# Second attention of a two-block model on one core: the differential heads' bias rows written out by GpSimd, so that VectorE adds bias and takes the maximum in one instruction per softmax

## The chip, the core and the metric

The kernel runs as one launch on one core of a Trainium2 chip. Its time is the device time of that core in microseconds (us); before and after are compared by their medians. The engines are TensorE (PE in the profile, PEld for its weight loads), VectorE (DVE), ScalarE (ACT), GpSimd (POOL) and SyncE (SP, which here only issues DMAs). Each works through its own queue in order and waits on semaphores.

## The reference, cut to what matters

A first block (sparse attention, memory attention, SwiGLU) and a second block follow each other. The second block has four MLA heads and then four differential heads. Of the latter, for one head and 128 queries (`Q_BLOCK`) against all 1024 keys:

```python
bucket = _t5_bucket_2(kpos[None, :] - qpos[:, None])
bias = jnp.moveaxis(table[bucket], -1, 0)
s = jnp.einsum('bqhmd,bkhmd->bmhqk', qblk, k).astype(jnp.float32) * scale + bias
p = jax.nn.softmax(s, axis=-1)
a = p[:, 0] - lam * p[:, 1]
return jnp.einsum('bhqk,bkhd->bqhd', a.astype(v.dtype), v)
```

The bucket depends only on key position minus query position, and it is constant once that distance is 128 or more on either side. So for 128 queries the bias varies over at most 384 keys (the block's own 128 and 128 on each side); to the left and to the right of them it is one number per head.

## The kernel before, in words

The stage is cut into 64 units: one head times 128 queries. Units 0 to 31 are the MLA heads, 32 to 63 the differential heads; I call the latter d0 to d31 here. Within a differential head the query block is i = 0 to 7. Four units form a group; a group's probabilities are transposed and multiplied with the values together.

A differential unit goes through the engines like this. TensorE writes the logits of both softmaxes (m = 0, 1) to PSUM (`ps`, function `logits`, L1915/L1916); each may start when VectorE has read the former unit's logits of the same m (semaphore `e_red`). VectorE adds the bias, writes the row to SBUF (`rows` for m = 0, `second` for m = 1) and takes the maximum (`maxima`, L3724). ScalarE takes both exponentials (L2742). VectorE forms the difference of the two rows (`difference`: reciprocal L3738, a 128x1 product L3739, the 128x1024 product and sum L3740; both of the latter read two SBUF operands). TensorE transposes the four rows of a group, once all four differences are there (L1930), ScalarE copies them (L2750), and TensorE multiplies them with the values (L1942). VectorE's order is written out by hand: the difference of unit u-1 stands behind the maxima of unit u, except at the first unit of a group, where it stands ahead of them.

In the MLA heads VectorE has another duty instead, the rounded rest of the transposed probabilities (`pt_lo`, L3759). The last MLA group's rests fall among the maxima of d1 to d3.

The bias of a head is a tile of 128x384 (`e_bias`, two buffers), brought by SP (L698). SP issues twelve half-tile loads of the head's queries and keys first (L695), then the bias; from the third differential head on it also waits until the head two before has been read (`e_red`). The far bias is a column of that tile read with stride 0. A row of 1024 keys is therefore two or three instructions: left of the near keys, right of them, and the near keys. i = 0, 1, 6 and 7 have two pieces, i = 2 to 5 have three. A short reduction over the pieces' maxima follows (L3729).

GpSimd splits weights and MLA operands into a rounded part and a rest: `w_hi` (L785) adds zero to `w_raw`, and `w_lo` (L788) subtracts. Behind the last MLA head it splits the first two slabs of the output projection `out_2`, and then waits for the third until the attention is over.

Of the kernel before, what the change touches and what calls it, by code (L numbers as in the profile page):

```python
# [21 lines left out]
ALU = mybir.AluOpType  # L22
AX = mybir.AxisListType

P = 128
D = 1024
KT = D // P
S = 1024
NT = S // P
# [28 lines left out]
TAKEN = -3e38  # L58
# [65 lines left out]
def program(nc, t):  # L124

    out = t["out"]
    with ExitStack() as ctx:
# [4 lines left out]
        KB = 1024  # L132
# [4 lines left out]
        BR = AR + 64 * KB  # L137
# [3 lines left out]
        def at(name, offset, shape, dt=F32):  # L141
            return nc.alloc_sbuf_tensor_at(name, shape, dt, offset=offset)
# [20 lines left out]
        zero = small("zero", [P, 1])  # L163
# [117 lines left out]
        second = [at(f"second{i}", tmp_at + 4 * KB * i, [P, S]) for i in range(2)]  # L281
        o_stage = at("o_stage", late_at, [P, HALF])
        inverses = at("inverses", late_at + 2 * KB, [P, 4, P])
        e_bias = at("e_bias", late_at + 4 * KB, [P, 2, 3 * P])
        e_stat = at("e_stat", late_at + 7 * KB, [P, 8, 6, 2])
        o_in = at("o_in", BR, [P, KT, S])
        o_rms = [at(f"o_rms{i}", BR + 40 * KB + 4 * KB * i, [P, S]) for i in range(2)]
# [22 lines left out]
        def wide(slot):  # L310

            return ps[:, 2 * slot:2 * slot + 2, :].rearrange("p b n -> p (b n)")
# [113 lines left out]
        def splits_before(hd):  # L426

            return 10 * hd
# [125 lines left out]
        def _(sp):  # L554
# [126 lines left out]
            for d in range(DIFF_HEADS):  # L681
                hd, p = MLA_HEADS + d, head_parts[d % 2]
                q_hi, q_lo = (t["diff_qk"][part, d] for part in range(2))
                k_hi, k_lo = (t["diff_qk"][part, d + DIFF_HEADS] for part in range(2))
                sp.wait_ge(a_qk, NT * (hd - 1) + NT * max(0, d - 1))
                sp.wait_ge(heads_in, heads_landed(hd))
                if d == 0:
                    sp.wait_ge(head_split, splits_before(MLA_HEADS))
                for dst, lanes, src in ((p[0], top, q_hi[top]), (p[0], bottom, q_lo[top]),
                                        (p[1], top, q_lo[bottom]), (p[1], bottom, q_hi[bottom]),  # L690
                                        (p[2], top, k_hi[top]), (p[2], bottom, k_hi[top]),
                                        (p[7], top, k_lo[top]), (p[7], bottom, k_lo[top]),
                                        (p[3], top, k_hi[bottom]), (p[3], bottom, k_hi[bottom]),
                                        (p[8], top, k_lo[bottom]), (p[8], bottom, k_lo[bottom])):
                    sp.dma_start(dst[lanes, :].bitcast(F32), src).then_inc(heads_in, 16)  # L695
                if d >= 2:
                    sp.wait_ge(e_red, 16 * (d - 1))
                sp.dma_start(e_bias[:, d % 2, :], t["bias_tiles_2"][d]).then_inc(bias_2_in[d % 2], 16)  # L698
                sp.wait_ge(a_pv, 16 * (hd - 1))
                sp.dma_start(v_plain[d % 2][:], t["diff_v"][d].rearrange("p j n -> p (j n)")).then_inc(heads_in, 16)  # L700
            load_slabs(SLABS["out_2"][0] + 2, N_SLABS)
# [77 lines left out]
        def _(pool):  # L779
# [29 lines left out]
            def split_front_first(n):  # L809

                s, front, back = n % 2, slice(0, HALF), slice(HALF, 1024)
                hi, lo = w_hi[s], w_lo[s]
                pool.wait_ge(raw_landed[s], loaded(n))
                pool.wait_ge(front_used, FRONT_FIRST.index(n) + 1)
                step(nc.gpsimd.tensor_tensor(hi[:, front], raw[s][:, front], zero[:, 0:1].broadcast_to([P, HALF]), ALU.add))  # L815
                nc.gpsimd.tensor_tensor(lo[:, front], raw[s][:, front], hi[:, front].bitcast(F32),
                                        ALU.subtract).then_inc(front_split, 1)
                pool.wait_ge(w_used, n - 1)
                nc.gpsimd.tensor_tensor(hi[:, back], raw[s][:, back], zero[:, 0:1].broadcast_to([P, HALF]),
                                        ALU.add).then_inc(w_rounded, 1)  # L820
                pool.wait_ge(w_rounded, n + 1)
                nc.gpsimd.tensor_tensor(lo[:, back], raw[s][:, back], hi[:, back].bitcast(F32),
                                        ALU.subtract).then_inc(w_split, 1)

            def split_next(n):

                pool.wait_ge(w_used, n - 1)
                pool.wait_ge(raw_landed[n % 2], loaded(n))
                split(n % 2, n + 1)
# [218 lines left out]
            for hd in range(MLA_HEADS):  # L1048
# [48 lines left out]
                pool.wait_ge(head_split, splits_before(hd) + 9)  # L1097
                rest(2, p[5], both)
            pool.wait_ge(head_split, splits_before(MLA_HEADS))
            first = SLABS["out_2"][0]  # L1100
            split_next(first)
            split_next(first + 1)
            split_front_first(first + 2)
            split_next(first + 3)
            split_slabs(first + 4, N_SLABS)
# [1911 lines left out]
        def _(dve):  # L3017
# [683 lines left out]
            def maxima(unit):  # L3701
                g, q, d = unit // 4 % 2, unit % 4, unit - NT * MLA_HEADS
                if d < 0:
                    dve.wait_ge(a_qk, unit + 1)
                    nc.vector.tensor_reduce(mstat[:, g, 1, q:q + 1], wide(unit % 2), AX.X, ALU.max,
                                            negate=True).then_inc(a_max, 1)
                    return

                i, bias = unit % NT, e_bias[:, d // NT % 2, :]
                if i == 0:  # L3710
                    dve.wait_ge(bias_2_in[d // NT % 2], 16 * (d // NT // 2) + 16)
                near0, near1 = max(0, i - 1) * P, min(NT, i + 2) * P
                b0 = P if i == 0 else 0
                stats = e_stat[:, unit % 8]
                dve.wait_ge(a_tr, 2 * (unit - unit % 4) - 8)
                if d >= 2:
                    dve.wait_ge(a_probs, d - 1)
                for m, row in enumerate((prob_rows[g][q], second[unit % 2])):
                    dve.wait_ge(a_qk, NT * MLA_HEADS + 2 * d + m + 1)
                    for kind, lo, hi, b in ((0, 0, near0, bias[:, 0:1].broadcast_to([P, near0])),  # L3720
                                            (2, near1, S, bias[:, 3 * P - 1:3 * P].broadcast_to([P, S - near1])),
                                            (1, near0, near1, bias[:, b0:b0 + near1 - near0])):
                        if lo < hi:
                            ins = nc.vector.tensor_tensor_reduce(row[:, lo:hi], wide(m)[:, lo:hi], b, 1.0, TAKEN,  # L3724
                                                                 ALU.add, ALU.max, stats[:, kind, m:m + 1])
                    ins.then_inc(e_red, 1)
                dve.wait_ge(e_red, 2 * d + 2)
                kinds = slice(0 if near0 else 1, 3 if near1 < S else 2)
                nc.vector.tensor_reduce(stats[:, 3, :], stats[:, kinds, :].rearrange("p k m -> p m k"), AX.X, ALU.max,  # L3729
                                        negate=True).then_inc(a_max, 1)  # L3730

            def difference(unit):

# [476 lines left out]
```

## Time and profile before

| what | value |
|---|---|
| median of 3 runs | 3044.64 us (3044.28 to 3047.01) |
| the profiled execution's own time | 3047.95 us |
| its span | 3046.2 us |
| TensorE busy | 2923.9 us (96%) |
| VectorE busy | 2043.8 us (67%) |
| GpSimd busy | 1607.7 us (53%) |
| differential units' maxima | from 2112.0 to about 2271.6 us of the span |

Busy shares are averages over stages with different limits, and TensorE's ends are modelled. All times of a row are in us from the span's start, durations in us unless marked ns. In a timeline, a bracket at a row's end is the time that the engine sat idle before it, and what ended it.

### The profile page before, as it was taken

Reading aid. Unit: us, or ns where it says so; the run is one execution under the profiler, and the core shown is the slowest. Engines: PE = TensorE matmul, PEld = TensorE weight load, DVE = VectorE, ACT = ScalarE, POOL = GpSimd, SP = SyncE. Lnnn points to the kernel's source line nnn. Section 1 sums busy time; section 2 is a strip of 40 time slices with the busy share of each in tenths; the row PEclk is TensorE's granted clock in tenths of the full one; section 3 lists DMA queues with packets and bytes.
Section 4 is the critical chain, followed back from the end, with each engine's and each line's share of the span. In section 5 each row is a group of like instructions: output and inputs, shape, how many; then the busy total and the mean of one; then the engine's idle time right before and its main releaser. Section 6 shows DMA issues by size and latency. Waiting matters only on the chain.

```text
span 3046.2 us, 39303 instructions
## 1 busy us (share of the span) xinstructions
PE 2923.9 (96%) x12850; PEld 2297.7 (75%) x12850; DVE 2043.8 (67%) x3010; ACT 1246.5 (41%) x2024; POOL 1607.7 (53%) x1015
## 2 busy tenths in 40 slices
PE   9999998999989999999999999999999899999998
PEld 7788775668877778887787677587657688877886
DVE  7899975546276977777548532456984766666658
ACT  4321215620246644444222432455774566652221
POOL 3254333324442388888679234471002477777877
PEclk9999999999999999999999999999999999999999
DMA  3122310025121144445974122624422277788774
GB/s 124 39 90 97 144 57 21 1 88 206 52 76 49 73 173 163 164 164 193 373 263 148 51 98 95 207 80 109 116 83 67 89 263 262 261 334 334 264 254 172
DMA packets 156608, 449.31 MB, mean 148 GB/s; under 512 B 17084, under 2 KB 28516, under 8 KB 155720
## 3 DMA queue, kind: packets, MB, share of 16 engines
q1 hardware_dynamic: 128656, 369.68, 34.9%
q10 hardware_dynamic: 27832, 78.08, 6.9%
q8 instruction: 69, 1.13, 0.2%
q14 instruction: 51, 0.42, 0.0%
HBM read 298.25 MB, written 148.13 MB: 147 GB/s over the span
## 4 chain that ended last, share of the span: by engine, by line
PE 74%; DVE 9%; issue 6%; POOL 5%; ACT 3%; DMA 2%; SPq 0%; ACTq 0%; POOLq 0%; DVEq 0%
PE ps L1223 21%; PE ps L1225 20%; PE ps L1224 20%; POOL left_lo L896 2%; PE ps L1466 2%; PE ps L1942 1%; PE ps L1930 1%; PE ps L1273 1%; POOL part_in L891 1%; DVE sums_t L3509 1%; PE ps L1456 1%; PE ps L1915 1%; PE ps L1916 1%; DVE score L3102 0%; DVE tmp L3040 0%
## 5 line engine op out<-in xcount | busy, mean ns | idle before, releaser
L896 POOL TENSOR_TENSOR left_lo<-part_in,left_hi 128x512 fp32r<-128x512 f32 x414 | 576.3, 1406 | 254.9 <-ACT left_hi L2843 89.6
L891 POOL TENSOR_TENSOR part_in<-part_in,part_in 128x512 f32<-128x512 f32 x252 | 364.0, 1445 | 35.8 <-DMA part_in<-mlp_weights_dram 15.0
L785 POOL TENSOR_TENSOR w_hi<-w_raw,zero 128x1024 fp32r<-128x1024 f32 x65 | 127.5, 1962 | 424.3 <-PE ps L1225 419.9
L1223 PE MATMUL ps<-h_hi,w_hi 128*128 128x512 f32 x480 | 188.4, 393 | 5.7 <-DVE h_lo L3034 5.7
L1224 PE MATMUL ps<-h_lo,w_hi 128*128 128x512 f32 x480 | 187.3, 390 | 0.0
L1225 PE MATMUL ps<-h_hi,w_lo 128*128 128x512 f32 x480 | 187.3, 390 | 0.0
L788 POOL TENSOR_TENSOR w_lo<-w_raw,w_hi 128x1024 fp32r<-128x1024 f32 x65 | 181.3, 2790 | 5.1
L3127 DVE MATCH_REPLACE8 score<-top,score 128x1024 f32<-128x1024 f32 (+2 forms) x192 | 180.5, 1020 | 0.0
L815 POOL TENSOR_TENSOR w_hi<-w_raw,zero 128x512 fp32r<-128x512 f32 x4 | 5.6, 1398 | 329.9 <-PE ps L1225 329.9
L1223 PE MATMUL ps<-down_t,left_hi 128*128 128x512 f32 x432 | 170.9, 396 | 8.4 <-DVE part_t L3414 4.1
L3123 DVE MAX8 top<-score 128x8 f32<-128x1024 f32 (+2 forms) x192 | 174.6, 1022 | 0.0
L1224 PE MATMUL ps<-down_t,left_hi 128*128 128x512 f32 x432 | 169.7, 393 | 0.0
L1225 PE MATMUL ps<-down_t,left_lo 128*128 128x512 f32 x432 | 169.6, 393 | 0.0
L2863 ACT ACTIVATE left_hi<-part_in 128x512 fp32r<-128x512 f32 x96 | 59.1, 630 | 201.8 <-PE ps L1225 175.6
L1223 PE MATMUL ps<-sums_hi,left_hi 128*128 128x512 f32 x320 | 126.4, 395 | 5.8 <-POOL left_lo L896 4.7
L2496 ACT ACTIVATE left_hi<-part_in 128x512 fp32r<-128x512 f32 x140 | 84.7, 626 | 104.0 <-DMA part_in<-ffn_weights_dram 40.3
L1225 PE MATMUL ps<-sums_hi,left_lo 128*128 128x512 f32 x320 | 125.3, 392 | 0.0
L1224 PE MATMUL ps<-sums_lo,left_hi 128*128 128x512 f32 x320 | 125.1, 391 | 0.0
L1223 PE MATMUL ps<-normed_hi,w_hi 128*128 128x512 f32 x272 | 116.7, 429 | 5.4 <-DVE normed_lo L3591 4.3
L1223 PEld LDWEIGHTS ps<-h_hi,w_hi 128*128 128x128 f32 x480 | 90.4, 188 | 26.5 <-DVE h_lo L3034 7.7
L876 POOL TENSOR_TENSOR mix_rows<-mix_rows,stat 128x128 f32<-128x128 f32 (+7 forms) x48 | 54.9, 1146 | 103.5 <-DVE stat L3168 103.4
L1224 PE MATMUL ps<-normed_lo,w_hi 128*128 128x512 f32 x272 | 106.7, 392 | 0.0
(640 smaller groups left out, 8739.4 us busy)
## 6 DMA issues: line engine op xcount, KB each, us to landing
w_raw<-weights_dram SPq DMA_DIRECT2D x102, 512.0 KB, 3.3
part_in<-ffn_weights_dram SPq DMA_DIRECT2D x144, 256.0 KB, 3.3
part_in<-mlp_weights_dram SPq DMA_DIRECT2D x144, 256.0 KB, 4.5
mlp_parts_scratch<-part_t SPq DMA_DIRECT2D x64, 512.0 KB, 4.7
down_t<-mlp_parts_scratch SPq DMA_DIRECT2D x64, 512.0 KB, 6.5
ffn_parts_scratch<-part_t SPq DMA_DIRECT2D x44, 512.0 KB, 4.7
down_t<-ffn_parts_scratch SPq DMA_DIRECT2D x44, 512.0 KB, 6.3
mlp_parts_scratch<-part_b SPq DMA_DIRECT2D x32, 512.0 KB, 5.1
```

Of the source, the lines that this page charges most:

```text
L785: nc.gpsimd.tensor_tensor(w_hi[s][:], raw[s][:], zero[:, 0:1].broadcast_to([P, 1024]), ALU.add).then_inc(w_rounded, 1)
L788: nc.gpsimd.tensor_tensor(w_lo[s][:], raw[s][:], w_hi[s][:].bitcast(F32), ALU.subtract).then_inc(w_split, 1)
L891: tt(part_in[p][dst][:], part_in[p][dst][:], part_in[p][other][:], ALU.add).then_inc(left_summed, 1)
L896: tt(lo[:], src[:], hi[:].bitcast(F32), ALU.subtract).then_inc(w_split, 1)
L1223: nc.tensor.matmul(out, sh, mh, start=start, stop=False)
L1224: nc.tensor.matmul(out, sh, ml, start=False, stop=False)
L1225: return nc.tensor.matmul(out, sl, mh, start=False, stop=stop)
L1466: nc.tensor.matmul(ps[:, 6 + group % 2, :], value[:, j, :], probs_t[n_tr % 2][:], start=j == 0, stop=j == group // 2).then_inc(pv_done, 1)
L2496: nc.scalar.activation(left[i % 4][0][:], part_in[p][RAW_OF_UP[i]][:], ACT.Copy).then_inc(w_rounded, 1)
L2863: nc.scalar.activation(left[j % 4][0][:], src[:], ACT.Copy).then_inc(w_rounded, 1)
L3123: nc.vector.max(top8[:, e, :], sc).then_inc(dve_step, 1)
L3127: nc.vector.match_replace(sc, top8[:, e, :], sc, TAKEN).then_inc(dve_step, 1)
```

## The change

`e_bias` becomes a full row of 2S - P = 1920 columns per head, at another place in SBUF. SP writes the same 384 columns, now into its middle (columns 768 to 1151). GpSimd fills the 768 columns on each side with the neighbouring column (`far_biases`), so that every query block i finds its 1024 bias values as one slice, from column (7 - i)·128 on. VectorE then needs one instruction per softmax, and the maxima of both are negated by a small multiplication instead of the reduction. A semaphore step of 18 instead of 16 makes VectorE wait for both fills. The fills of heads 0 and 1 stand on GpSimd's queue ahead of the first two slabs of `out_2`, those of heads 2 and 3 behind them.

```diff
-        e_bias = at("e_bias", late_at + 4 * KB, [P, 2, 3 * P])
+        BIAS_SPAN, NEAR_AT = 2 * S - P, S - 2 * P
+        e_bias = at("e_bias", BR + 36 * KB, [P, 2, BIAS_SPAN])
...
-                sp.dma_start(e_bias[:, d % 2, :], t["bias_tiles_2"][d]).then_inc(bias_2_in[d % 2], 16)
+                sp.dma_start(e_bias[:, d % 2, NEAR_AT:NEAR_AT + 3 * P], t["bias_tiles_2"][d]).then_inc(bias_2_in[d % 2], 16)
...
+            def far_biases(d):
+
+                e = d % 2
+                pool.wait_ge(bias_2_in[e], 18 * (d // 2) + 16)
+                for lo, hi, col_of in ((0, NEAR_AT, NEAR_AT), (NEAR_AT + 3 * P, BIAS_SPAN, NEAR_AT + 3 * P - 1)):
+                    nc.gpsimd.tensor_tensor(e_bias[:, e, lo:hi], e_bias[:, e, col_of:col_of + 1].broadcast_to([P, hi - lo]),
+                                            zero[:, 0:1].broadcast_to([P, hi - lo]), ALU.add).then_inc(bias_2_in[e], 1)
+
+            far_biases(0)
+            far_biases(1)
             first = SLABS["out_2"][0]
             split_next(first)
             split_next(first + 1)
+            far_biases(2)
+            far_biases(3)
             split_front_first(first + 2)
...
-                    dve.wait_ge(bias_2_in[d // NT % 2], 16 * (d // NT // 2) + 16)
-                near0, near1 = max(0, i - 1) * P, min(NT, i + 2) * P
-                b0 = P if i == 0 else 0
+                    dve.wait_ge(bias_2_in[d // NT % 2], 18 * (d // NT // 2) + 18)
+                row0 = (NT - 1 - i) * P
...
-                    for kind, lo, hi, b in ((0, 0, near0, bias[:, 0:1].broadcast_to([P, near0])),
-                                            (2, near1, S, bias[:, 3 * P - 1:3 * P].broadcast_to([P, S - near1])),
-                                            (1, near0, near1, bias[:, b0:b0 + near1 - near0])):
-                        if lo < hi:
-                            ins = nc.vector.tensor_tensor_reduce(row[:, lo:hi], wide(m)[:, lo:hi], b, 1.0, TAKEN,
-                                                                 ALU.add, ALU.max, stats[:, kind, m:m + 1])
-                    ins.then_inc(e_red, 1)
+                    nc.vector.tensor_tensor_reduce(row[:], wide(m), bias[:, row0:row0 + S], 1.0, TAKEN,
+                                                   ALU.add, ALU.max, stats[:, 1, m:m + 1]).then_inc(e_red, 1)
                 dve.wait_ge(e_red, 2 * d + 2)
-                kinds = slice(0 if near0 else 1, 3 if near1 < S else 2)
-                nc.vector.tensor_reduce(stats[:, 3, :], stats[:, kinds, :].rearrange("p k m -> p m k"), AX.X, ALU.max,
-                                        negate=True).then_inc(a_max, 1)
+                ts(stats[:, 3, :], stats[:, 1, :], -1.0, None, ALU.mult).then_inc(a_max, 1)
```

GpSimd's queue behind the last MLA head (`head_part` is that head's last split, `w_hi`/`w_lo` the slabs of `out_2`), before:

```order
L1068 TENSOR_TENSOR head_part_5_231<-head_raw_214,head_part_4_230 128x1024 [waits head_split]
L785 TENSOR_TENSOR w_hi_51<-w_raw_49,zero 128x1024 [waits raw_landed0,w_used,head_split]
L788 TENSOR_TENSOR w_lo_53<-w_raw_49,w_hi_51 128x1024 [waits w_rounded]
L785 TENSOR_TENSOR w_hi_52<-w_raw_50,zero 128x1024 [waits raw_landed1,w_used]
L788 TENSOR_TENSOR w_lo_54<-w_raw_50,w_hi_52 128x1024 [waits w_rounded]
L815 TENSOR_TENSOR w_hi_51<-w_raw_49,zero 128x512 [waits front_used,raw_landed0]
```

And the same place of the queue after:

```order
L1069 TENSOR_TENSOR head_part_5_231<-head_raw_214,head_part_4_230 128x1024 [waits head_split]
L1107 TENSOR_TENSOR e_bias<-e_bias,zero 128x768 [waits bias_2_in0,head_split]
L1107 TENSOR_TENSOR e_bias<-e_bias,zero 128x768
L1107 TENSOR_TENSOR e_bias<-e_bias,zero 128x768 [waits bias_2_in1]
L1107 TENSOR_TENSOR e_bias<-e_bias,zero 128x768
L786 TENSOR_TENSOR w_hi_51<-w_raw_49,zero 128x1024 [waits raw_landed0,w_used]
L789 TENSOR_TENSOR w_lo_53<-w_raw_49,w_hi_51 128x1024 [waits w_rounded]
L786 TENSOR_TENSOR w_hi_52<-w_raw_50,zero 128x1024 [waits raw_landed1,w_used]
L789 TENSOR_TENSOR w_lo_54<-w_raw_50,w_hi_52 128x1024 [waits w_rounded]
L1107 TENSOR_TENSOR e_bias<-e_bias,zero 128x768 [waits bias_2_in0]
```

The two slabs' splits (four instructions) now stand behind the second head's bias (`bias_2_in1`), so they cannot start before its load has landed.

VectorE's queue at d3, a unit with three pieces per row (`rows_3` is m = 0, `second_252` is m = 1; the 128x1 rows write the maximum out), before:

```order
L3724 ISA rows_3_246,e_stat<-ps,e_bias 128x256 [waits attn_logits,attn_probs,attn_transposed]
L3724 ISA e_stat 128x1
L3724 ISA rows_3_246,e_stat<-ps,e_bias 128x384
L3724 ISA e_stat 128x1
L3724 ISA rows_3_246,e_stat<-ps,e_bias 128x384
L3724 ISA e_stat 128x1
L3724 ISA second_252,e_stat<-ps,e_bias 128x256 [waits attn_logits]
```

And from the same unit after, on to the differences of d2 and d3 and the first row of d4:

```order
L3733 ISA rows_3_246,e_stat<-ps,e_bias 128x1024 [waits attn_logits,attn_probs,attn_transposed]
L3733 ISA e_stat 128x1
L3733 ISA second_252,e_stat<-ps,e_bias 128x1024 [waits attn_logits]
L3733 ISA e_stat 128x1
L3736 TENSOR_SCALAR e_stat<-e_stat 128x2 [waits attn_biased]
L3765 TENSOR_TENSOR pt_lo<-ps,pt_hi 128x512 [waits attn_probs_t_hi] x2
L3744 RECIPROCAL e_stat<-e_stat 128x1 [waits attn_exp]
L3745 SCALAR_TENSOR_TENSOR e_stat<-e_stat,stat 128x1 [waits dve_step]
L3746 SCALAR_TENSOR_TENSOR rows_2_245<-second_251,e_stat,rows_2_245 128x1024 [waits dve_step]
L3744 RECIPROCAL e_stat<-e_stat 128x1 [waits attn_exp]
L3745 SCALAR_TENSOR_TENSOR e_stat<-e_stat,stat 128x1 [waits dve_step]
L3746 SCALAR_TENSOR_TENSOR rows_3_246<-second_252,e_stat,rows_3_246 128x1024 [waits dve_step]
```

Six pieces of the unit became two instructions of 1024 columns; what stands behind them keeps its order.

## Rows read from the trace of the kernel before

**Rows 1.** The page: share of the chain that ended last, by engine.

```profile
PE 74%; DVE 9%; issue 6%; POOL 5%; ACT 3%; DMA 2%; SPq 0%; ACTq 0%; POOLq 0%; DVEq 0%
```

**Rows 2.** The chain in order of time, d2 to d4: start, duration, what.

```profile
2120.58 1.29 DVE pt_lo L3759 x2
...
2139.52 0.50 PE ps L1915
```

**Rows 3.** The same chain, at a later group's first unit (d12).

```profile
2176.69 0.55 DVE rows L3724
...
2180.62 1.72 PE ps L1942 x4
```

**Rows 4.** Timeline of VectorE, from d1's difference to d4: start, duration, instruction.

```profile
2127.82 0.22 DVE L3739 SCALAR_TENSOR_TENSOR e_stat<-e_stat,stat 128x1 f32<-128x1 f32 x1
2128.08 1.28 DVE L3740 SCALAR_TENSOR_TENSOR rows<-second,e_stat,rows 128x1024 f32<-128x1024 f32 x1
2129.50 0.42 DVE L3724 CUSTOM_DVE_ANT_0 rows<-ps,e_bias 128x256 f32<-128x256 f32 x1
...
2130.80 0.42 DVE L3724 CUSTOM_DVE_ANT_0 second<-ps,e_bias 128x256 f32<-128x256 f32 x1
...
2136.78 0.55 DVE L3724 CUSTOM_DVE_ANT_0 rows<-ps,e_bias 128x384 f32<-128x384 f32 x1
...
2175.03 0.16 DVE L3738 RECIPROCAL e_stat<-e_stat 128x1 f32<-128x1 f32 x1 [1.23 <-ACT second L2742]
```

**Rows 5.** Groups by shape, VectorE, 2100 to 2290: count, busy us, mean ns.

```profile
L3724 DVE CUSTOM_DVE_ANT_0 rows<-ps,e_bias 128x384 f32<-128x384 f32 x32 | 17.4, 552 | 0.0
L3724 DVE CUSTOM_DVE_ANT_0 rows<-ps,e_bias 128x768 f32<-128x768 f32 x8 | 7.6, 954 | 0.5
```

**Rows 6.** Timeline of TensorE: the longer idle times, and value products behind the last.

```profile
2136.93 1.09 PE L1930 MATMUL ps<-ident,rows 128*128 128x128 f32 x8 [1.68 <-DVE rows L3740]
2276.64 1.09 PE L1930 MATMUL ps<-ident,rows 128*128 128x128 f32 x8 [2.09 <-DVE rows L3740]
2278.07 3.48 PE L1942 MATMUL ps<-pt_plain,v_plain 128*128 128x512 f32 x4 [0.34 <-ACT pt_plain L2750]
```

**Rows 7.** Windows of 1 us: length, busy of five engines, granted clock, DMA.

```profile
2278.00:2279.00 1.00, 0.93 (x1) 0.50 (x2) 0.00 (x0) 0.42 (x1) 0.00 (x0) 0.50 1.03 418
```

**Rows 8.** SP's timeline at the second head's bias; its load's row, KB, us to landing.

```profile
2115.85 0.59 SPq L698 DMA_DIRECT2D e_bias<-bias_tiles_scratch  x1
e_bias<-bias_tiles_scratch SPq DMA_DIRECT2D x1, 192.0 KB, 10.0
```

**Rows 9.** Timeline of GpSimd: the second slab's split, and a 128x512 rounding.

```profile
2067.39 1.90 POOL L785 TENSOR_TENSOR w_hi<-w_raw,zero 128x1024 fp32r<-128x1024 f32 x1
2069.38 2.41 POOL L788 TENSOR_TENSOR w_lo<-w_raw,w_hi 128x1024 fp32r<-128x1024 f32 x1
2311.17 1.04 POOL L815 TENSOR_TENSOR w_hi<-w_raw,zero 128x512 fp32r<-128x512 f32 x1 [239.39 <-PE ps L1225]
```

**Rows 10.** Timelines of VectorE and GpSimd near 1831, and the same VectorE instruction alone.

```profile
1830.30 1.90 POOL L785 TENSOR_TENSOR w_hi<-w_raw,zero 128x1024 fp32r<-128x1024 f32 x1 [7.54 <-PE ps L1225]
1831.31 1.97 DVE L3660 TENSOR_TENSOR d_out<-d_out,d_hi 128x1024 f32<-128x1024 f32 x1
1832.27 3.23 POOL L788 TENSOR_TENSOR w_lo<-w_raw,w_hi 128x1024 fp32r<-128x1024 f32 x1
...
1864.56 1.22 DVE L3660 TENSOR_TENSOR d_out<-d_out,d_hi 128x1024 f32<-128x1024 f32 x1 [1.13 <-ACT d_hi L2683]
```

**Rows 11.** Short instructions beside GpSimd; by line: ns min/median/max, first and last start.

```profile
494.95 0.83 POOL L876 TENSOR_TENSOR mix_rows<-mix_rows,stat 128x384 f32<-128x384 f32 x1 [2.93 <-DVE stat L3168]
495.47 0.32 DVE L3163 TENSOR_TENSOR stat<-stat 128x1 f32<-128x1 f32 x1
...
L3164 DVE TENSOR_SCALAR stat<-stat x64: 153/154/156, 476.5 to 634.6; 128x1 f32<-128x1 f32 x64
L3759 DVE TENSOR_TENSOR pt_lo<-ps,pt_hi x64: 680/682/693, 1986.2 to 2132.9; 128x512 fp32r<-128x512 f32 x64
```

## The prediction

> **What bounds the kernel now.** I read the page's chain first: TensorE holds 74% of it, VectorE 9% [rows 1]. The change touches only the differential heads, so I followed the chain in order of time through that stage. It has two kinds of stretch. From d2 to d4 it lies on VectorE without a break, from the first `pt_lo` at 2120.58 to the logits that TensorE starts at 2139.52 [rows 2]: the last MLA group's rests and three units of maxima come together there, and TensorE waits, 1.68 us ahead of the first differential group's transposes [rows 6]. Later TensorE sets the pace inside a group, and only the step from one group to the next runs over the others: ScalarE's exponentials, the difference, then both rows of the next unit's maxima, until TensorE has its second logits and goes on to the values [rows 3]. There VectorE is idle for 1.23 us for the last exponential [rows 4], so what it saves earlier in a group is worth nothing. On the path are thus the maxima of d2, d3, d4 and of the first unit of each of six more groups (d8, d12, ... d28).
>
> **What one instruction per row saves.** The pieces of 384 and 768 columns take 552 and 954 ns [rows 5], that is 1.047 ns per column; the 768 are read with stride 0 and the 384 are not, and I take it that both stream alike. A row of three pieces takes 2130.80 - 2129.50 = 1.30 us from start to start [rows 4]; of this 1024 x 1.047 = 1.07 us are columns, so each piece costs 0.077 us beside them. One instruction takes 1.07 + 0.077 = 1.15 us. It saves 0.15 us against three pieces and 0.08 against two, per row. The differential heads lose 160 - 64 = 96 instructions, 7.4 us of VectorE time, but on the path lie only: d2, d3 and d4 with three pieces, 3 x 2 x 0.154 = 0.92 us; d12, d20, d28 likewise 0.92 us; d8, d16, d24 with two pieces, 3 x 2 x 0.077 = 0.46 us. Together 2.3 us. The reduction against the small multiplication I put at nothing: a negation of one column takes 154 ns [rows 11], hardly less than a short VectorE instruction in general.
>
> The Trainium skill ("VectorE: DVE Perf Modes", section on the TRN2 errata) gives a PSUM-to-SBUF instruction 120 cycles of fixed cost at 0.96 GHz, 0.125 us. By that the 30 instructions taken off the path would be an estimated 3.75 us instead of 2.3. The trace shows 0.077 from start to start, and the sum goes by the trace.
>
> **What GpSimd's new work costs.** This is the larger term. The trace shows a VectorE instruction with two SBUF operands waiting for GpSimd: L3660 takes 1.22 us alone, and 1.97 when it starts at 1831.31 while `w_hi` runs; it ends at 1833.28, 1.08 us behind the end of `w_hi` (1832.20), as though it began only there. GpSimd's next instruction in turn takes 3.23 instead of 2.41 us [rows 9, 10]. The 128x1 L3163 that starts at 495.47 ends with GpSimd's instruction (495.78 against 495.79) [rows 11]. With one operand in PSUM nothing waits: L3759 stays within 680 to 693 ns over a stretch with and without GpSimd [rows 11]. So the maxima, which read PSUM, are safe, but L3739 and L3740 of each difference are not. Before, GpSimd is idle throughout the differential heads, for it did its two slabs from about 2063 on [rows 9] and its next instruction waits 239 us [rows 9].
>
> The Trainium skill ("SBUF — State Buffer", section on who interferes with whom) says that VectorE with two SBUF inputs and a GpSimd instruction that reads SBUF exclude each other for the whole instruction, whichever started first. The trace agrees, 1.97 against 1.22 us.
>
> Now the timing. The second head's bias is issued at 2115.85 and takes 10.0 us to land [rows 8], at about 2125.9. Its two fills of 768 columns lie between 1.04 us (512) and 1.90 (1024) of a rounding with stride-0 zero [rows 9]; I take 1.47 each. They run 2125.9 to 2128.9, and the moved slab splits follow at once: the first `w_hi` 2129.0 to 2130.9. All this falls into VectorE's unbroken stretch. Step by step (before: [rows 4]):
> - d1's L3739, due at 2127.5 (0.3 earlier than before), is held to 2128.9. L3740 comes at 2129.2, finds `w_hi`, and ends at 2130.9 + 1.08 = 2132.0, against 2129.36 before.
> - d3's two rows (2.3), the negation (0.2), two `pt_lo` (1.2) and the reciprocal (0.2) bring L3739 of d2 to 2136.0. Meanwhile `w_lo` started at 2132.0 and ended at 2134.3, the second `w_hi` runs to 2136.3. L3739 waits for it; L3740 then finds the second `w_lo` (to 2138.7) and ends at 2139.8.
> - d3's difference adds 1.6, so d4's first row starts at about 2141.4 instead of 2136.78, and TensorE's second logits start at 2141.4 + 2.3 = 2143.7 instead of 2139.52: 4.2 us later, with the 0.9 gained in d2 to d4 already taken off.
>
> If the fills were as fast as the nearest lower row (1.04) it would be about 3.4; if they landed half a microsecond later, about 4.5.
>
> The fills of heads 2 and 3 meet groups in which TensorE leads. Each pair lasts 3 us and can hold one L3740 by up to 1.4 us; most of it hides in the 1.23 us for which VectorE waits there [rows 4]. I take 0.4 us each (0 to 1.4), 0.8 together. The first head's fills meet only MLA maxima and `pt_lo`, all from PSUM: nothing. The `out_2` slabs are needed after the attention; their splits end near 2139, and the next one is started at 2311 [rows 9].
>
> Last, the clock. TensorE will be idle for about 4 us behind d3's logits and again for about 4 before the transposes of the first differential group, where its longest idle time was 1.68 [rows 6]. Behind an idle time of 2.09 us at 2276.64 the granted clock went to 0.50 (1.2 GHz) [rows 6, 7], and four value products took 3.48 us instead of 1.72 [rows 3, 6]. A fall like that costs up to 1.7 us if it meets TensorE at work, nothing if it falls into the wait. I take 1.0.
>
> **Sum**: + 4.2 + 0.8 + 1.0 - 1.4 (d8 to d28) = + 4.6 us. Against the profiled execution (3047.95 us, span 3046.2) that makes 3052.6; against the median of the runs, which is 3.3 us lower, 3049.2.
>
> **The rivals.**
> 1. *No collision that counts*: the saving alone, 2.3 us, gives 3042.3. It needs the fills, whose sources are stride-0 columns, not to hold VectorE, and the splits to run beside single-input work. Against it: `w_hi` has such a source too and does hold, and the four splits alone last 2 x (1.90 + 2.41) = 8.6 us of a stretch in which VectorE has no idle time.
> 2. *The negation is held as well*. It now treats two columns, and its reductions before were of another kind. For d2 and d3 it could meet a fill or a split and delay the exponentials too: some 0.6 to 2.1 us more, about 3050.7. Against it: 64 negations of one column never took over 156 ns, though GpSimd worked in that stretch [rows 11]. The Trainium skill (the same section of "SBUF — State Buffer") lets a tensor_scalar take the shared pair when it runs in a 2-port mode; no row here shows one of two columns.
> 3. *Clearly faster*: if VectorE's 7.4 us all came off the stage, 3037.2. That would need VectorE to set the pace inside the groups; its 1.23 us of idle time at the group's end [rows 4] and TensorE's unbroken work speak against it. It decides only if TensorE waits in most units, where it now waits once per group.
>
> **How the numbers follow.** A measurement of this kernel tells about 0.2% (6.1 us) from no change. Chances: the forecast 0.62, rival 2 0.20, rival 1 0.14, rival 3 0.04. The forecast's own range is + 2 (fast fills, clock fall hidden) to + 7 (late landing 0.3, clock 0.7, both later pairs 1.4 at most). It passes 6.1 in about 1 of 7 cases, rival 2 in about 2 of 3, so slower 0.22; rival 3 leaves 0.03 for faster; the rest, 0.75, is no change that can be told. The range 3042.6 to 3052.0 leaves out most of rival 3, part of rival 1 and the tail of rival 2.
>
> **What the changed kernel's profile would show.** The 64 rows as single instructions near 1.22 us. GpSimd's fills at 2126 to 2129 and the splits behind them to about 2139. L3740 (now L3746) above 1.28 us for d1 and d2, near 3 us each, ending about 1.08 behind a GpSimd instruction, and one slightly held in heads 2 and 3. The first group's transposes near 2141.5 instead of 2136.93 with an idle time of about 4 us, and a fall of the granted clock near it. Group steps 0.15 to 0.3 us shorter. The prediction is wrong if L3746 stays at 1.28 beside GpSimd, if the fills last far less than 1 us, or if the bias lands before 2123 or after 2130.

## The result and the profile after

| | before | changed |
|---|---|---|
| median of 20 runs each | 3047.24 us (3042.22 to 3052.36) | 3053.27 us (3048.55 to 3058.4) |
| profiled execution | 3047.95 us | 3054.55 us |
| its span | 3046.2 us | 3052.8 us |
| VectorE instructions | 3010 | 2818 |

The ratio is 1.0016, with a 95% interval from 1.0010 to 1.0022: the changed kernel is slower by 3.0 to 6.7 us, 4.9 in the middle. (It is not the quotient of the two medians, which lie 6.03 us apart.) The forecast was + 4.6 us. Its absolute number, 3049.2, and its range up to 3052.0 missed the median of 3053.27, mostly because the level of the kernel before had been read from three runs (3044.64), which lie 2.6 us below the median of twenty.

The timeline of VectorE in the changed kernel, from d1's difference to d4 (columns as in [rows 4]; maxima's writes left out):

```profile
2125.84 1.22 DVE L3733 CUSTOM_DVE_ANT_0 rows<-ps,e_bias 128x1024 f32<-128x1024 f32 x1
2126.99 1.22 DVE L3733 CUSTOM_DVE_ANT_0 second<-ps,e_bias 128x1024 f32<-128x1024 f32 x1
2128.25 1.33 DVE L3736 TENSOR_SCALAR e_stat<-e_stat 128x2 f32<-128x2 f32 x1
2129.50 1.28 DVE L3765 TENSOR_TENSOR pt_lo<-ps,pt_hi 128x512 fp32r<-128x512 f32 x2
2130.70 0.15 DVE L3744 RECIPROCAL e_stat<-e_stat 128x1 f32<-128x1 f32 x1
2130.88 0.22 DVE L3745 SCALAR_TENSOR_TENSOR e_stat<-e_stat,stat 128x1 f32<-128x1 f32 x1
2131.14 2.81 DVE L3746 SCALAR_TENSOR_TENSOR rows<-second,e_stat,rows 128x1024 f32<-128x1024 f32 x1
...
2136.49 1.56 DVE L3736 TENSOR_SCALAR e_stat<-e_stat 128x2 f32<-128x2 f32 x1
...
2139.34 1.18 DVE L3745 SCALAR_TENSOR_TENSOR e_stat<-e_stat,stat 128x1 f32<-128x1 f32 x1
2140.55 1.28 DVE L3746 SCALAR_TENSOR_TENSOR rows<-second,e_stat,rows 128x1024 f32<-128x1024 f32 x1
...
2143.40 1.22 DVE L3733 CUSTOM_DVE_ANT_0 rows<-ps,e_bias 128x1024 f32<-128x1024 f32 x1
```

And GpSimd's timeline in the same kernel, the fills and the moved splits:

```profile
2128.09 2.89 POOL L1107 TENSOR_TENSOR e_bias<-e_bias,zero 128x768 f32<-128x768 f32 x2 [34.89 <-DMA e_bias<-bias_tiles_scratch]
2130.94 1.92 POOL L786 TENSOR_TENSOR w_hi<-w_raw,zero 128x1024 fp32r<-128x1024 f32 x1
2132.94 3.22 POOL L789 TENSOR_TENSOR w_lo<-w_raw,w_hi 128x1024 fp32r<-128x1024 f32 x1
2136.13 1.89 POOL L786 TENSOR_TENSOR w_hi<-w_raw,zero 128x1024 fp32r<-128x1024 f32 x1
2138.09 2.41 POOL L789 TENSOR_TENSOR w_lo<-w_raw,w_hi 128x1024 fp32r<-128x1024 f32 x1
```

Read the two side by side; L3736 is the negation, L3745 the short product of a difference (128x1) and L3746 the long one (128x1024). L3746 starts at 2131.14, finds the first `w_hi` (2130.94 to 2132.86) and ends at 2133.95, 1.09 us behind it. L3745 at 2139.34 waits for the second `w_lo`, which ends at 2140.50. And the short negation L3736, 0.17 us by itself, takes 1.33 and 1.56 us: it ends at 2129.58 and 2138.05, where the first fill (2128.09 + 1.46 = 2129.55) and the second `w_hi` (2138.02) end. GpSimd waits in turn: the first `w_lo` takes 3.22 us instead of 2.41, for it starts at 2132.94 while L3746 runs. Nothing that reads PSUM is touched: both rows take 1.22 us, `pt_lo` is unchanged.

This execution ran 2.19 us late already when d0 began (2114.16 against 2111.97). The delay is older than the change: the last MLA head's split starts at 2060.80 against 2058.60, ahead of the first instruction that differs. So I compare distances. In the table "step d0" is from the start of d0's first row on VectorE to that of d4, and so on through the first units of the groups; "d0 to d28" is their sum. Each number is a difference of two starts in VectorE's timeline of that kernel. Free steps in the changed kernel are 19.7 us.

| step from | d0 | d4 | d8 | d12 | d16 | d20 | d24 | d0 to d28 |
|---|---|---|---|---|---|---|---|---|
| before | 24.81 | 20.03 | 19.88 | 20.02 | 19.88 | 20.02 | 19.88 | 144.52 |
| changed | 29.24 | 20.84 | 20.48 | 19.71 | 20.68 | 19.71 | 19.70 | 150.36 |

TensorE's rows that answer to [rows 6] and the changed kernel's clock, in a window of 1 us (columns as in [rows 7]):

```profile
2135.36 0.50 PE L1929 MATMUL ps<-head_part,head_part 128*128 128x512 f32 x1 [2.60 <-DVE e_stat L3733]
...
2143.54 1.37 PE L1944 MATMUL ps<-ident,rows 128*128 128x128 f32 x8 [2.75 <-DVE rows L3746]
...
2285.82 1.95 PE L1956 MATMUL ps<-pt_plain,v_plain 128*128 128x512 f32 x4 [0.34 <-ACT pt_plain L2764]
...
2145.00:2146.00 1.00, 1.00 (x3) 0.81 (x3) 0.96 (x4) 0.55 (x1) 0.00 (x0) 0.50 0.00 0
```

The granted clock fell to 0.50 (1.2 GHz) behind the two waits of 2.60 and 2.75 us; the fall was forecast, the waits at about 4 us each. But at the stage's end, where before four value products took 3.48 us [rows 6], they now take 1.95: there the clock did not fall (it is 1.00 from 2284 to 2287). From d28's first row to VectorE's last scaling of a head's output (L3755 before, L3761 now) it is 33.31 us against 35.12. The whole stage, d0 to that instruction, is thus 5.84 - 1.81 = 4.03 us longer.

### The profile page after: what moved, and what is told of

It is laid out like the page before. It is cut to its first block, busy times and chain, and to the rows that moved or that the text cites. A ratio compares the mean times of both kernels' runs of the same rounds, so it can differ in the third digit from the quotient of the medians.

```text
span 3052.8 us, 39120 instructions
## 1 busy us (share of the span) xinstructions
PE 2926.0 (96%) x12850; PEld 2299.3 (75%) x12850; DVE 2044.8 (67%) x2818; ACT 1247.1 (41%) x2024; POOL 1621.5 (53%) x1023
## 4 chain that ended last, share of the span: by engine, by line
PE 62%; issue 12%; POOL 11%; DVE 9%; ACT 3%; DMA 2%; SPq 0%; POOLq 0%; ACTq 0%; DVEq 0%
PE ps L1237 17%; PE ps L1238 16%; PE ps L1239 16%; POOL left_lo L897 7%; POOL part_in L892 3%; PE ps L1480 2%; PE ps L1944 1%; PE ps L1287 1%; PE ps L1956 1%; PE ps L1470 1%; DVE sums_t L3523 1%; PE ps L1929 1%; DVE rows L3733 1%; PE ps L1930 1%; DVE score L3116 0%
## 5 line engine op out<-in xcount | busy, mean ns | idle before, releaser
L3141 DVE MATCH_REPLACE8 score<-top,score 128x1024 f32<-128x1024 f32 (+2 forms) x192 | 170.8, 918 | 0.0
L3137 DVE MAX8 top<-score 128x8 f32<-128x1024 f32 (+2 forms) x192 | 165.0, 922 | 0.0
```

Of the source, the lines that this page charges most:

```text
L3137: nc.vector.max(top8[:, e, :], sc).then_inc(dve_step, 1)
L3141: nc.vector.match_replace(sc, top8[:, e, :], sc, TAKEN).then_inc(dve_step, 1)
```

## The experiments

Times are medians, the ratio is to the kernel before on the same chip (e1 to e4 ran on one chip, e5 to e8 on another). The interval of about 0.09% on either side tells less than the distances in the traces, so verdicts rest on the latter. Each trace is one execution, and d0 to d28 leaves out the stage's end, where a fall of the clock comes and goes. What the times do show: e7 is slower than the kernel before, and the interval of e2 lies wholly below that of the changed kernel (1.0010 to 1.0022), so the order of GpSimd's queue alone takes the loss away.

| kernel | time | ratio (95%) | step d0 | later steps with fills | d0 to d28 |
|---|---|---|---|---|---|
| e1 negation by reduction | 3049.27 | 1.0000 (0.9991 to 1.0009) | 28.78 | 20.58, 20.18 | 148.43 |
| e2 splits first | 3046.44 | 0.9997 (0.9988 to 1.0006) | 25.35 | 20.63, 20.30 | 145.12 |
| e3 no fills | 3045.77 | 0.9995 (0.9986 to 1.0004) | 24.19 | none | 143.82 |
| e4 fills by ScalarE | 3046.94 | 0.9997 (0.9988 to 1.0006) | 24.19 | 19.92, 19.95, 19.91 | 143.16 |
| e5 e1 and e2 together | 3046.00 | 0.9997 (0.9988 to 1.0006) | 25.07 | 19.87, 19.87 | 143.68 |
| e6 old rows, late splits | 3049.24 | 1.0006 (0.9997 to 1.0015) | 28.47 | none | 148.17 |
| e7 old rows, all fills | 3052.88 | 1.0020 (1.0010 to 1.0030) | 29.14 | 20.66, 20.53 | 151.26 |
| e8 memsets for fills | 3045.96 | 0.9996 (0.9987 to 1.0005) | 24.21 | 19.72, 19.71 | 142.50 |

An edit shifts line numbers. The text names the negation, the short and the long product by the changed kernel's lines (L3736, L3745, L3746); the rows in the fences carry the numbers of their own kernel.

The traces together show what a held instruction costs. I call "held" what the negations and the two products of a step take beyond their 0.17, 0.22 and 1.28 us. A step without fills and with one instruction per row takes 24.19 us from d0 and 19.71 later (e3); with rows in pieces it is 24.81 and 19.88 (before).

| kernel | held in step d0 | unheld step + held | step d0 | held, heads 2 and 3 | their steps above a free one |
|---|---|---|---|---|---|
| changed | 5.04 | 29.23 | 29.24 | 1.96, 2.14 | 0.77, 0.97 |
| e1 | 4.60 | 28.79 | 28.78 | 2.07, 1.69 | 0.87, 0.47 |
| e2 | 1.15 | 25.34 | 25.35 | 2.09, 1.78 | 0.92, 0.59 |
| e5 | 0.88 | 25.07 | 25.07 | 1.37, 1.38 | 0.16, 0.16 |
| e6 | 3.64 | 28.45 | 28.47 | none | none |
| e7 | 4.31 | 29.12 | 29.14 | 1.22, 1.09 | 0.78, 0.65 |

In step d0 every held microsecond is paid. Later 1.2 us of it are free (0.44 with rows in pieces) and the rest is paid, whichever instruction is held. VectorE's timeline in the changed kernel shows where they go, first the step of head 2, then a free step:

```profile
2174.15 1.03 DVE L3736 TENSOR_SCALAR e_stat<-e_stat 128x2 f32<-128x2 f32 x1
...
2175.28 1.32 DVE L3745 SCALAR_TENSOR_TENSOR e_stat<-e_stat,stat 128x1 f32<-128x1 f32 x1
...
2183.06 0.17 DVE L3744 RECIPROCAL e_stat<-e_stat 128x1 f32<-128x1 f32 x1 [0.80 <-ACT second L2756]
...
2202.78 0.16 DVE L3744 RECIPROCAL e_stat<-e_stat 128x1 f32<-128x1 f32 x1 [1.99 <-ACT second L2756]
```

VectorE's wait for the group's last exponential shrinks from 1.99 to 0.80 us, and it is 0.80 in every step of these kernels with a fill that holds (1.23 and 0.80 with rows in pieces).

**e1.** Does the held negation cost by itself?

```diff
-                ts(stats[:, 3, :], stats[:, 1, :], -1.0, None, ALU.mult).then_inc(a_max, 1)
+                nc.vector.tensor_reduce(stats[:, 3, :], stats[:, 1:2, :].rearrange("p k m -> p m k"), AX.X, ALU.max,
+                                        negate=True).then_inc(a_max, 1)
```

> The changed kernel, but both maxima are negated by the short reduction of before (over one column per softmax) instead of the small multiplication. 'd0 to d28' is the time from the start of d0's first row on VectorE to the start of d28's first row: 144.5 us before, 150.4 changed. Theory A (GpSimd's instructions hold every VectorE instruction with two SBUF inputs; the negation's holding only moved the same wait): the negation drops from up to 1.56 to 0.16 us each, but the difference behind it meets GpSimd instead, so d0 to d4 stays near 29.0 us (24.8 before, 29.2 changed), and heads 2 and 3 lose less than the 0.8 and 1.0 of the changed kernel, some 0.4 each: d0 to d28 about 149.3, time 0.5 to 1 us below the changed kernel. Rival B (the held negation is what costs, because the exponentials wait for it): d0 to d4 falls to 26.5 or less and d0 to d28 to 147 or less.

Step d0 is 28.78, near theory A's 29.0 and far from B's 26.5. The reductions are not held; instead L3745 of d1 (it takes 1.16 us) and L3746 of d1 and d2 are (2.88 and 3.35 us), nearly the sequence of the forecast. In step d0 the held negation thus costs 0.46 us by itself (29.24 - 28.78). The loss of 0.4 us each for heads 2 and 3 came to 0.87 and 0.47. The median came out 4.9 us below the changed kernel in ratio, more than the 0.5 to 1 expected, while d0 to d28 is 1.93 less; 1.1 of that is the step from d4 (19.74 against 20.84), for here the clock fell at 2132, during TensorE's wait, and was back at 1.00 before the transposes at 2141.55. The two ratios have intervals of 2.7 and 1.8 us on either side, so the 4.9 is uncertain by about 3.3 and does not contradict 1.93; besides, the traced execution (3053.4) was the slowest of e1's eleven. How much of the time's difference is the negation's stays open.

**e2.** What do the moved splits make, and what the fills?

```diff
-            far_biases(0)
-            far_biases(1)
             first = SLABS["out_2"][0]
             split_next(first)
             split_next(first + 1)
+            far_biases(0)
+            far_biases(1)
             far_biases(2)
```

> The changed kernel, but the two slabs of out_2 are split ahead of all fills, as before; the fills stay. Theory A (the moved splits make most of the loss): only 2.9 us of fills meet VectorE's unbroken stretch, one negation is held by about 1.3 us and no L3746 is, so d0 to d4 is 24.8 - 0.9 + 1.2 = 25.1 us instead of 29.2; TensorE's idle time there falls under 2 us and the clock does not fall near it. d0 to d28 about 145.3, time within 0.05% of the kernel before. Rival B (the fills themselves make most of it): d0 to d4 stays above 27 us, d0 to d28 above 147.

Theory A holds, at 25.35 and 145.12 against 25.1 and 145.3 expected. VectorE's timeline of e2 at d2:

```profile
2125.99 1.32 DVE L3736 TENSOR_SCALAR e_stat<-e_stat 128x2 f32<-128x2 f32 x1
...
2128.60 0.22 DVE L3745 SCALAR_TENSOR_TENSOR e_stat<-e_stat,stat 128x1 f32<-128x1 f32 x1
2128.86 1.28 DVE L3746 SCALAR_TENSOR_TENSOR rows<-second,e_stat,rows 128x1024 f32<-128x1024 f32 x1
```

Only the negation meets a fill; the short product behind it starts at 2128.60, and the second fill ends at 2128.71. TensorE waits 1.68 us ahead of the transposes, and the granted clock stays at 1.00 from 2130 to 2150. Putting the four split instructions in front of all eight fills takes 3.9 us from step d0 and, since no fall of the clock came there in this execution, another 1.1 from the next one.

**e3.** The saving alone (the far bias is left out):

```diff
+            for e in range(2):
+                for lo, hi in ((0, NEAR_AT), (NEAR_AT + 3 * P, BIAS_SPAN)):
+                    nc.gpsimd.memset(e_bias[:, e, lo:hi], 0.0).then_inc(bias_2_in[e], 1)
```

> The changed kernel without any fill: GpSimd sets the far columns of both bias buffers to zero once, behind the last MLA split, so the far bias is left out of the sums; the slabs are split first and the maxima are negated by the reduction. This is the one instruction per row alone. Theory A (the saving is 0.15 us per row against three pieces, 0.08 against two, and only the rows of d2 to d4 and of each later group's first unit are on the path): d0 to d28 144.5 - 2.0 = 142.5 us (2.3 less with d28's own rows), time 0.1% or less below the kernel before. Rival C (all 7.4 us of VectorE time come off): d0 to d28 about 138.

Step d0 falls by 0.62 (0.6 was expected up to d4's start, where d2 and d3 count), the free steps by 0.31 and 0.17. In this execution the clock fell at 2139 and made the step from d4 21.08 instead of 19.7; without that d0 to d28 would be about 142.5. e8 below, without a fall there, shows 142.50. Rival C is ruled out.

**e4.** Fills on an engine that holds nobody:

```diff
+            def far_bias(d, side):
+                e, (lo, hi, at_col) = d % 2, ((0, NEAR_AT, NEAR_AT), (NEAR_AT + 3 * P, BIAS_SPAN, NEAR_AT + 3 * P - 1))[side]
+                act.wait_ge(bias_2_in[e], 18 * (d // 2) + 16 + side)
+                nc.scalar.activation(e_bias[:, e, lo:hi], e_bias[:, e, at_col:at_col + 1].broadcast_to([P, hi - lo]),
+                                     ACT.Copy).then_inc(bias_2_in[e], 1)
...
+                    if n in (1, 2) and 6 <= group <= 12 and group % 2 == 0:
+                        far_bias(group // 2 - 3, n - 1)
```

> The whole computation, with the slabs split first, the maxima negated by the reduction, and the fills made by ScalarE, one in each of two units ahead of the head's first use (in group 6 for head 0, 8, 10, 12 for heads 1 to 3). Theory A: ScalarE holds nobody, each fill takes about 0.87 us (between 0.60 for 512 and 1.15 for 1024 columns) and lies in a unit in which ScalarE waits 0.8 us or more, so the stage is that of the kernel without fills, d0 to d28 about 142.5 to 143.5, time 0.05% to 0.1% below the kernel before. Rival D (ScalarE's exponentials are too near the path): each fill delays its unit, up to 6 x 0.87 us, d0 to d28 up to 148.

ScalarE's two fills of head 1 in the timeline of e4:

```profile
2148.06 0.83 ACT L2766 ACTIVATE e_bias<-e_bias 128x768 f32<-128x768 f32 x1
...
2153.19 0.84 ACT L2766 ACTIVATE e_bias<-e_bias 128x768 f32<-128x768 f32 x1
```

No product and no reduction of VectorE is held in e4. The steps that hold two fills are 19.92, 19.95 and 19.91, 0.2 us over free ones, for 1.67 us of ScalarE work. This is the whole computation at 143.16, within the expected 142.5 to 143.5 and 1.4 us below the kernel before. As a time it is not told from it (0.9997).

**e5.** Both corrections, fills still on GpSimd.

> The changed kernel with both corrections at once: slabs split first, maxima negated by the reduction; the fills stay on GpSimd. Theory A: the negation meets nothing, so d1's short difference L3739 is held instead, by about 1.1 us as in the first experiment; d0 to d4 is 24.2 + 1.1 = 25.3 us, the steps of heads 2 and 3 with fills stay at 20.6 and 20.2 against 19.7 free ones; d0 to d28 about 145.0, the same as with the splits first alone (145.1). Rival B (the held negation costs on its own): d0 to d28 at 144.2 or less.

Step d0 is 25.07 (L3745 of d1 takes 1.10 us), as theory A had it. The later steps with fills are 19.87 instead of 20.6 and 20.2, and so d0 to d28 is 143.68, in rival B's range. It does not show rival B's cause. VectorE's instructions are the same in e1, where the steps are 20.58 and 20.18; what differs is when the fills come. In e5 head 2's start 9.1 us behind d8's first row (2165.41 against 2156.30), in e1 9.8 us (2170.95 against 2161.14). L3746 takes 2.45 us in both, but L3745 in front of it only 0.42 in e5 and 1.12 in e1. So 1.37 us are held instead of 2.07, 1.2 of them are free, and 0.16 is paid instead of 0.87. Nor do the traces show that a free negation shortens these steps by itself: with it e1 holds 2.07 and 1.69 us, without it the changed kernel 1.96 and 2.14 and e2 2.09 and 1.78.

**e6.** The moved splits alone, on the kernel before:

```diff
             pool.wait_ge(head_split, splits_before(MLA_HEADS))
+            pool.wait_ge(bias_2_in[1], 16)
             first = SLABS["out_2"][0]
```

> The kernel before with one wait added: GpSimd splits the first two out_2 slabs only when the second head's bias has landed. No fills, rows in two or three pieces. Theory A (the moved splits alone hold VectorE's differences): w_hi from 2125.9, w_lo to about 2130.3, so d1's L3740 ends about 2.0 us late, later ones hardly; d0 to d4 about 26.9 us instead of 24.8; d0 to d28 about 146.6 (plus up to 1.1 if the clock falls at the first differential group), time 0.07% above the kernel before. Rival B (a late split is harmless without the fills ahead of it): d0 to d4 stays at 24.8.

Rival B is ruled out. Theory A's direction holds, but the size is 3.66 us, not 2.1. The timelines of e6, VectorE and GpSimd:

```profile
2128.37 2.26 DVE L3740 SCALAR_TENSOR_TENSOR e_stat<-e_stat,stat 128x1 f32<-128x1 f32 x1
2130.66 2.88 DVE L3741 SCALAR_TENSOR_TENSOR rows<-second,e_stat,rows 128x1024 f32<-128x1024 f32 x1
...
2126.25 1.89 POOL L785 TENSOR_TENSOR w_hi<-w_raw,zero 128x1024 fp32r<-128x1024 f32 x1 [62.73 <-DMA e_bias<-bias_tiles_scratch]
2128.22 2.39 POOL L788 TENSOR_TENSOR w_lo<-w_raw,w_hi 128x1024 fp32r<-128x1024 f32 x1
2130.56 1.90 POOL L785 TENSOR_TENSOR w_hi<-w_raw,zero 128x1024 fp32r<-128x1024 f32 x1
```

My 2.1 us had the short product pass just ahead of `w_lo`. It came 0.15 us behind the start of `w_lo` (2128.37 against 2128.22) and ended with it (2130.63 against 2130.61), and the long one then found the next `w_hi`. An estimate of such a collision is thus no better than the estimate of the starts: here 0.15 us decided about 2.

**e7.** All fills and the moved splits, but rows in two or three pieces and the reduction as before, the near piece read from the middle of the wide buffer.

> The changed kernel's fills, order of GpSimd's queue and wide bias buffer, but VectorE's rows in two or three pieces and the reduction as before: the collision without the saving. Theory A: d0 to d4 is 24.8 + 4.6 = 29.4 us, steps with fills 0.5 to 0.9 above 20.0 and 20.0; d0 to d28 about 150.5 (up to 1.1 more if the clock falls at work), time 0.2% above the kernel before. Rival B (it is the wide rows that suffer): d0 to d28 stays below 147.

Step d0 is 29.14 and d0 to d28 151.26, of which about 0.95 is a fall of the clock in the step from d4 (20.98 against a free 20.03); with the ratio of 1.0020 this is as theory A had it. The loss is that of GpSimd's work, and the wide rows have no part in it. Nor does the new place of the bias buffer: the steps without fills (20.03 and 19.89) are those of the kernel before.

**e8.** Does GpSimd hold VectorE by writing, too? Splits first; each fill is four memsets to zero (the far bias is left out):

```diff
+                    if lo:
+                        pool.wait_ge(bias_2_in[e], 18 * (d // 2) + 17)
+                    for again in range(3):
+                        step(nc.gpsimd.memset(e_bias[:, e, lo:hi], 0.0))
+                    nc.gpsimd.memset(e_bias[:, e, lo:hi], 0.0).then_inc(bias_2_in[e], 1)
```

> The changed kernel with the slabs split first, and each fill replaced by four memsets to zero in a row (so the far bias is left out), some 6 us of GpSimd writing SBUF and reading none per head; the negation stays the small multiplication. If only GpSimd instructions that read SBUF hold VectorE's instructions with two SBUF inputs (the Trainium skill says so in SBUF - State Buffer, section on who interferes with whom), no L3745 or L3746 is held, though several run beside memsets, and steps with fills come down to 19.7. If any GpSimd instruction holds them, L3746 takes up to 2 us. The negation, held in the changed kernel, may be held here by writes or not: by up to 0.75 us (a memset of 768 columns took 0.74 alone) if it uses the shared pair for its output too. d0 to d4 24.2 to 25.0, d0 to d28 142.5 to 144.

The timelines of e8 at head 2, VectorE and GpSimd:

```profile
2166.93 0.22 DVE L3748 SCALAR_TENSOR_TENSOR e_stat<-e_stat,stat 128x1 f32<-128x1 f32 x1
2167.18 1.28 DVE L3749 SCALAR_TENSOR_TENSOR rows<-second,e_stat,rows 128x1024 f32<-128x1024 f32 x1
...
2171.01 0.56 DVE L3739 TENSOR_SCALAR e_stat<-e_stat 128x2 f32<-128x2 f32 x1
...
2166.02 2.34 POOL L1110 MEMSET e_bias<- 128x768 f32 x3 [33.13 <-DMA e_bias<-bias_tiles_scratch]
2168.41 0.74 POOL L1111 MEMSET e_bias<- 128x768 f32 x1
2169.21 2.33 POOL L1110 MEMSET e_bias<- 128x768 f32 x3
```

The long product with two SBUF inputs runs 1.28 us amid the memsets. The two-column negation is held: five of the six that run beside a memset take 0.42 to 0.65 us, less than one memset (0.74). It costs nothing: in step d0 (24.21) the `pt_lo` behind a held negation still starts its usual 0.08 us after it (2126.98 against 2126.90), and the later holds of 0.40 and 0.95 us stay under the 1.2 that are free. The Trainium skill ("SBUF — State Buffer", section on who interferes with whom) has both: two SBUF inputs contend only with a GpSimd instruction that reads SBUF, and a tensor_scalar in a 2-port mode with any. The trace agrees (1.28 us beside a writer, 2.81 in the changed kernel beside a reader; 0.56 for the negation beside a writer).

## Why the prediction was right, and where it was wrong

The failed step is the last of the sum: "against the median of the runs, which is 3.3 us lower, 3049.2". It took the three runs of before (3044.64) for the level, and they happened to lie low; twenty have a median of 3047.24 and spread over 10 us. That is 2.6 of the 4.0 us by which 3053.27 lies above 3049.2. On the level of twenty the forecast would have been 3051.8. The range took in the bounds of the costs and nothing for the level. The other 1.4 us is the change itself, 6.0 us by the medians (4.9 by the ratio, 3.0 to 6.7) against the forecast 4.6. Its mis-sized term is "I take 0.4 us each" for the fills of heads 2 and 3, which cost 0.77 and 0.97; and the negation, whose difference from the reduction "I put at nothing", cost 0.46 in step d0. That the sum came so near is partly luck: these errors were offset by a clock fall that stayed away at the stage's end.

Its steps, one by one:
- **The saving**: right. One instruction takes 1.22 us and steps 1.15 us on; free group steps are 0.31 and 0.17 us shorter (0.31 and 0.15 forecast), step d0 0.62 (e3, e4). VectorE's other saved time came to nothing (rival 3 is out).
- **GpSimd holds VectorE**: right. e2 and e6 show it from both sides, e7 shows that it is independent of the saving. The held times account for step d0 within 0.02 us in six kernels.
- **The landing and the fills**: the load landed at 2128.09 - 2.19 = 2125.90 on the clock of before (2125.9 forecast), and a fill takes 1.46 us (1.47).
- **The collision at d1 to d3**: size right, sequence wrong, so the size owes something to luck. Step d0 grew by 4.43 us (5.04 held less 0.62 saved); the forecast put d4's first row 4.6 late. But the holding that rival 2 named came true, without its 0.6 to 2.1 us: the negation was held, by 1.16 and 1.39 us over its 0.17. That pushed d2's long product past the last `w_lo`, and only one of the forecast two was held (2.81 us). The one held wait took the other's place but for 0.46 us, as e1 shows: with the negation free both long products are held, and the step is 28.78. The argument from 64 one-column negations does not carry over to two columns, and it was thinner than it looked: only 11 of the 64 ran beside a GpSimd instruction.
- **The fills of heads 2 and 3**: mis-sized, 0.77 and 0.97 us over the free 19.71 instead of 0.4 each. The forecast let a pair hold one long product by up to 1.4 us and most of it hide in a wait of 1.23. In fact a pair held the negation and the short product, 1.96 and 2.14 us together, and 1.2 of it was free.
- **The clock**: the fall beside the first differential group came and cost 20.84 - 19.74 = 1.10 us (1.0 taken; the 19.74 is e1's, whose clock fell earlier). TensorE's waits around it were 2.60 and 2.75 us, not about 4. But at the stage's end a fall was absent, worth 1.81 - 0.31 = 1.5 us there, so that over the stage the clock took nothing. I had added the first and kept the second.

Put together, with the steps of the trace: 4.43 + 0.81 + 0.60 - 0.31 + 0.80 - 0.31 - 0.18 - 1.81 = 4.03 us from d0 to the stage's end. The span grew by 6.6; 2.19 of it lie ahead of d0, older than the change, and 0.4 behind the stage, where nothing was changed. Both belong to these two executions and can't be put to the change.

What stays open: how much of the time between e1 and the changed kernel is the negation's, and what decides whether the clock falls at the stage's end. It is not a fall ahead of it: e7 had both, e2 neither. Nor is it the wait: TensorE is idle for 2.09 us ahead of the last group's transposes in all ten kernels alike, and the clock fell there in all but the changed kernel, e2 and e3. With one trace of each kernel, it isn't shown that the change has anything to do with it.

## What to carry to other kernels

Before moving work to GpSimd, list what VectorE runs beside it: here instructions with two SBUF inputs waited for the end of a GpSimd instruction that reads SBUF, and a tensor_scalar of two columns for that of any, while those with an input in PSUM passed. Look at what is queued behind the new wait as well: here the late place of the four slab splits, which nobody was waiting for, cost more (5.2 us of d0 to d28 with one fall of the clock, changed against e2) than the fills themselves (2.6, e2 against e8). A held VectorE instruction is paid in full where VectorE sets the pace and only beyond its waiting time where another engine does. And when a stage is paced by another engine, count only the instructions on its path: 96 instructions were saved, and the steps from d0 to d28 became 2.0 us shorter (e8), not 7.4.

## What the runs showed of the hardware that I had not expected

- A tensor_scalar of 128x2 is held by GpSimd (up to 1.56 us instead of 0.17), also by a memset (0.65); the one-column ones of the first attention never were (156 ns at most in 64, [rows 11], of which 11 ran beside GpSimd). The reduction over the same two columns never took over 156 ns in e1's and e5's 64, seven of them beside a fill or a split.
- GpSimd's memset of 128x768, which only writes, took 0.74 us and held none of the eight products with two SBUF inputs that ran beside it (0.22 and 1.28 us); a fill of the same size that reads a stride-0 column took 1.46 us and held such products (up to 2.45 us in e1 and e5, 1.32 for the short one in the changed kernel).
- A held product ends 1.08 to 1.09 us behind GpSimd's instruction if it is 128x1024, against 1.28 us by itself, and 0.02 us behind it if it is 128x1, against 0.22.
- Falls of the granted clock to 0.50 (1.2 GHz) come and go at the same place, behind the same idle time of 2.09 us. One is worth 1.1 to 1.5 us when it meets TensorE at work, more than half of the 2.0 us that the change saves from d0 to d28.
